# Four banks for the masked products of a recurrent chunk, its recurrence in one run, and the router within the output projection

## The reference

```python
def wkv7_scan(r, w, k, v, a, b):
    ...
        sa = jnp.einsum('bhij,bhj->bhi', state, a_t)
        state = (state * w_t[:, :, None, :] + sa[..., None] * b_t[:, :, None, :]
                 + v_t[..., None] * k_t[:, :, None, :])
        return state, jnp.einsum('bhij,bhj->bhi', state, r_t)
...
for i in range(DEPTH):
    ...
        mixed = jnp.concatenate([tok, mem_out.astype(tok.dtype)], axis=-1) @ w_out[i]
        x = layer_norm(DEEPNORM_ALPHA * x + mixed, ln1_g[i], ln1_b[i])
        ffn = moe_ffn(x.reshape(B_ * S_, D), w_router[i], router_bias[i], ...)
        x = layer_norm(DEEPNORM_ALPHA * x + ffn, ln2_g[i], ln2_b[i])
# in moe_ffn:
    scores = jax.nn.sigmoid((x2 @ w_router).astype(jnp.float32))
    _, idx = lax.top_k(scores + router_bias.astype(jnp.float32), TOP_K)
    ...
    shared = (jax.nn.silu(x2 @ w_sh_gate) * (x2 @ w_sh_up)) @ w_sh_down
```

## Time and profile before

| | us |
|---|---|
| median of 3 runs | 2351.93 (2348.82 to 2356.43) |
| the profiled execution | 2349.78 |
| its span | 2348.0 |
| PE busy | 2004.9 (85%) |
| DVE busy | 828.0 (35%) |
| DMA, mean rate | 230 GB/s |

### The profile page before, as it was taken

The page is one execution under the profiler, slowest core; times in us unless marked ns, Lnnn a source line. Parts: engine busy times, 40 slices in busy tenths (PEclk is TensorE's granted clock), DMA queues, the critical chain, the costliest instruction groups (busy, mean ns, idle before and its releaser), DMA issues. The chain is left out here.

```text
span 2348.0 us, 33222 instructions
## 1 busy us (share of the span) xinstructions
PE 2004.9 (85%) x11180; PEld 1226.0 (52%) x11181; DVE 828.0 (35%) x2198; ACT 361.7 (15%) x814; POOL 289.8 (12%) x375
## 2 busy tenths in 40 slices
PE   8999998798989887878897688988779897888885
PEld 5475545365655555533444377763446564554552
DVE  2001645422223222272545743313523232222236
ACT  1001631011101100012334211110101010100010
POOL 5000000011111111100134131000011111111110
PEclk9999999799989999998998599879889899998998
DMA  6211003699999999861222100002758999999966
GB/s 210 77 54 39 34 19 151 239 365 421 414 418 379 412 421 421 347 232 50 59 54 50 23 2 1 1 1 90 284 188 326 421 395 410 412 421 421 417 279 250
DMA packets 143456, 540.51 MB, mean 230 GB/s; under 512 B 30854, under 2 KB 68286, under 8 KB 93590
## 3 DMA queue, kind: packets, MB, share of 16 engines
q1 hardware_dynamic: 122070, 489.14, 52.0%
q0 software_dynamic: 21312, 50.37, 5.7%
HBM read 521.07 MB, written 45.61 MB: 241 GB/s over the span
## 5 line engine op out<-in xcount | busy, mean ns | idle before, releaser
L594 PE MATMUL bank<-W,XT 128*64 128x256 f32 x4608 | 569.1, 409 | 116.2 <-DMA W<-in_w_exp_up_dram 108.0
L594 PEld LDWEIGHTS bank<-W,XT 128*64 128x64 f32 x4608 | 413.2, 148 | 296.7 <-issue 197.9
L629 PE MATMUL bank<-W,ht 128*64 128x512 f32 x1152 | 263.1, 597 | 12.2 <-DVE ht L618 12.0
L647 POOL DMA_INDIRECT y_rows<-y,row x72 | 72.9, 1013 | 943.1 <-DVE y L640 943.1
L605 DVE TENSOR_TENSOR gu<-sig,bank 128x256 f32<-128x256 f32 x72 | 30.4, 422 | 409.5 <-ACT sig L601 409.5
L1733 PE MATMUL bank<-XT,rin_w 128*128 128x512 f32 x352 | 161.5, 615 | 0.0
L629 PEld LDWEIGHTS bank<-W,ht 128*64 128x64 f32 x1152 | 90.9, 136 | 127.0 <-issue 127.0
L1087 PE MATMUL bank<-XT,foxw 128*128 128x512 f32 x320 | 139.9, 599 | 0.0
L1733 PEld LDWEIGHTS bank<-XT,rin_w 128*128 128x128 f32 x352 | 68.6, 198 | 88.7 <-issue 88.4
L535 DVE TENSOR_TENSOR onehot<-rank,iota_s 128x128 bf16 x320 | 71.9, 287 | 97.9 <-issue 97.9
L601 ACT ACTIVATE sig<-bank 128x256 f32<-128x256 f32 x72 | 27.7, 384 | 508.5 <-PE bank L594 508.5
(11 more groups left out here) (390 smaller groups left out, 2395.9 us busy)
## 6 DMA issues: line engine op xcount, KB each, us to landing
W<-in_w_exp_gate_dram SPq DMA_DIRECT2D x128, 1024.0 KB, 14.6
W<-in_w_exp_up_dram SPq DMA_DIRECT2D x128, 1024.0 KB, 19.2
W<-in_w_exp_down_dram SPq DMA_DIRECT2D x128, 1024.0 KB, 17.9
W<-y_rows SPq DMA_DIRECT2D x16, 1536.0 KB, 17.6
foxw<-in_fox_w_in_dram SPq DMA_DIRECT2D x13, 1024.0 KB, 5.5
rin_w<-in_rwkv_w_in_dram SPq DMA_DIRECT2D x22, 512.0 KB, 4.0
w_out<-in_w_out_dram SPq DMA_DIRECT2D x1, 4096.0 KB, 13.2
x_rows<-X SPq DMA_DIRECT2D x2, 2048.0 KB, 16.4
```

The costliest lines, as they stand in the source:

```text
L594: last = pe.matmul((gate, up)[m][64 * a:64 * a + 64, :], xt[s][:, k, 64 * a:64 * a + 64], K.W[:, w, a, m, k * FE:(k + 1) * FE], start=(k = ...
L629: last = pe.matmul(B[5 + half][64 * a:64 * a + 64, :], ht[:, j, 64 * a:64 * a + 64], K.W[:, w, a, 2, at:at + 512], start=(j == 0), stop=(j ...
L647: pool.indirect_dma_start(out=K.y_rows, out_offset=bass.IndirectOffsetOnAxis(ap=row[s][:], axis=0), in_=y[s][:], in_offset=None, bounds_ch ...
```

## The change

Four things.

1. `a_products` puts pairs of heads in turn into banks 3 and 4 and banks 5 and 6 (`mask_bank`). A pair waits for the masks of the pair before the last.
2. In iteration c PE does z, the L products, deviations, u, variances, state and y, and then x5, spread, bonus, tw5, gate and x6. The lists of ACT and DVE are put in the same order.
3. Transposes and logits move from routing into the output projection, tile by tile, with `TileTurner` through banks 0 and 1 and logits in bank 2. Tile 0 is transposed before the products of tile 3; the others follow the products. The router's weights and the layer norm's vectors lie in the arena, and X is stored by tiles.
4. The shared expert's gate and down weights are loaded in the output projection (`SharedExpert`), so that routing loads only the router's bias and the up weights before the experts' weights.

```diff
@@ routed_experts_tables, sync
-                sp.dma_start(w_router[:], K.in_["w_router"][L].rearrange("(p k) e -> p k e", k=KD)).then_inc(loaded, 16)
                 sp.dma_start(bias[:, 0, :], K.in_["router_bias"][L:L + 1, :].broadcast_to([P, E])).then_inc(loaded, 16)
-                sp.dma_start(w_sh[:, 0, :], K.in_["w_sh_gate"][L].rearrange("(p k) f -> p (k f)", k=KD)).then_inc(loaded_sh, 16)
-                sp.dma_start(w_sh[:, 1, :], K.in_["w_sh_up"][L].rearrange("(p k) f -> p (k f)", k=KD)).then_inc(loaded_sh, 16)
-                shared.load(sp)
-                sp.dma_start(K.x_rows.rearrange("(t p) d -> p t d", p=P), X[:]).then_inc(stored, 16)
+                sp.dma_start(w_up[:], K.in_["w_sh_up"][L].rearrange("(p k) f -> p (k f)", k=KD)).then_inc(up_loaded, 16)
...
@@ routed_experts_tables, vector
-                dve.wait_ge(loaded, 32)
+                dve.wait_ge(loaded, 16)
                 dve.wait_ge(negexp_done, 1)
...
@@ TileTurner.turn
         pe.wait_ge(ln.done, 2 * t + 2)
+        if t:
+            pe.wait_ge(self.by_act, 2 * t)
...
@@ output_projection, sync
                 ln.load(sp)
+                sp.dma_start(router, K.in_["w_router"][L].rearrange("(p k) e -> p k e", k=KD)).then_inc(router_loaded, 16)
+                shared.load(sp)
+                for t in range(NT):
+                    sp.wait_ge(ln.done, 2 * t + 2)
+                    sp.dma_start(K.x_rows[t * P:(t + 1) * P, :], X[:, t, :]).then_inc(K.x_stored, 16)
@@ output_projection, tensor
+                def logits(t):
+                    tiles.await_tile(pe, t)
+                    if t == 0:
+                        pe.wait_ge(router_loaded, 16)
+                    for k in range(KD):
+                        pe.matmul(B[2][:, t * E:(t + 1) * E], K.XT[:, k, t * P:(t + 1) * P], router[:, k, :],
+                                  start=(k == 0), stop=(k == KD - 1))
...
+                    if t == 2:
+                        tiles.turn(pe, ln, 0)
+                logits(0)
+                for t in range(1, NT):
+                    tiles.turn(pe, ln, t)
+                    logits(t)
@@ output_projection, scalar
                 for t in range(NT):
                     ln.root(act, t)
+                    if t == NT - 2:
+                        tiles.copy(act, 0)
+                for t in range(1, NT):
+                    tiles.copy(act, t)
@@ rwkv_chunks
+        def mask_bank(h):
+            return B[3 + 2 * (h // 2 % 2) + h % 2]
...
         def a_products(pe, n, h0):
-            for h in (h0, h0 + 1):
-                if h >= 2:
-                    pe.wait_ge(a_kept, n * NH + h - 1)
-                elif n >= 2:
-                    pe.wait_ge(outs, n - 1)
-                elif n:
-                    pe.wait_ge(tok_k, 4 * n)
+            if h0 >= 4:
+                pe.wait_ge(a_kept, n * NH + h0 - 2)
+            elif n and h0 == 2:
+                pe.wait_ge(y_kept, 2 * n)
+            elif n >= 2:
+                pe.wait_ge(outs, n - 1)
+            elif n:
+                pe.wait_ge(tok_k, 4 * n)
@@ rwkv_chunks, tensor, iteration c
-                    if n < NT:
-                        x5(n)
                     u(c)
                     if c:
                         variances(c - 1)
                     if n < NT:
-                        tw5(n)
+                        state(c)
+                    y(c)
+                    if n < NT:
+                        x5(n)
                     if c:
                         spread_rstd(c - 1)
+                        bonus(c - 1)
                     if n < NT:
-                        state(c)
-                    if c:
-                        bonus(c - 1)
-                    y(c)
-                    if n < NT:
-                        x6(n)
+                        tw5(n)
                     if c:
                         gate(c - 1)
                     if n < NT:
+                        x6(n)
@@ rwkv_chunks, vector, iteration c
-                    for q in range(2 * GROUPS):
-                        if n < NT:
-                            add_tw5(n, q)
-                        if c and q == 1:
-                            invert_root(c - 1)
                     if c:
-                        scale_deviations(c - 1)
+                        invert_root(c - 1)
                     if n < NT:
                         update_state(c)
                     if c:
+                        scale_deviations(c - 1)
                         add_bonus(c - 1)
+                    if n < NT:
+                        for q in range(2 * GROUPS):
+                            add_tw5(n, q)
+                    if c:
                         gate_out(c - 1)
```

More of the change, by code:

```diff
@@ L283, in _, with shared_products @@
                             load_expert(K, sp, L, 2 * i + a, i, a, m)
-                sp.wait_ge(stored, 16)
+                sp.wait_ge(K.x_stored, 16 * NT * (L + 1))
             @block.tensor
             def _(pe):
-                for k in range(KD):
-                    if k >= 4:
-                        pe.wait_ge(xt_a if k % 2 == 0 else xt_d, (k - 4) // 2 + 1)
-                    for t in range(NT):
-                        last = pe.transpose(B[k % 4][:, t * P:(t + 1) * P], K.Xk[:, t, k, :], ident[:])
-                    last.then_inc(turned, 1)
-                pe.wait_ge(loaded, 32)
-                pe.wait_ge(xt_a, KD // 2)
-                pe.wait_ge(xt_d, KD // 2)
-                for t in range(NT):
-                    for k in range(KD):
-                        last = pe.matmul(B[4][:, t * E:(t + 1) * E], XT[:, k, t * P:(t + 1) * P], w_router[:, k, :],
-                                         start=(k == 0), stop=(k == KD - 1))
-                last.then_inc(logits, 1)
-                pe.wait_ge(loaded_sh, 32)
-                def shared_products(gu, j):
-                    for k in range(KD):
-                        last = pe.matmul(B[gu * 2 + j][:], w_sh[:, gu, k * FE + j * P:k * FE + (j + 1) * P],
+                def shared_products(gu, j):
+                    weights = w_up if gu else shared.gate
+                    if gu:
+                        pe.wait_ge(up_loaded, 16)
+                    else:
+                        pe.wait_ge(shared.gate_loaded, 16)
+                    for k in range(KD):
+                        last = pe.matmul(B[gu * 2 + j][:], weights[:, k * FE + j * P:k * FE + (j + 1) * P],
                                          XT[:, k, :], start=(k == 0), stop=(k == KD - 1))
@@ L346, in _ @@
             def _(act):
-                for k in range(0, KD, 2):
-                    act.wait_ge(turned, k + 1)
-                    act.activation(XT[:, k, :], B[k % 4][:], ACT.Copy).then_inc(xt_a, 1)
-                act.wait_ge(logits, 1)
-                act.activation(negexp[:], B[4][:, 0:NT * E].rearrange("p (t e) -> p t e", t=NT), ACT.Exp, scale=-1.0).then_inc(negexp_done, 1)
+                act.activation(negexp[:], B[2][:, 0:NT * E].rearrange("p (t e) -> p t e", t=NT), ACT.Exp, scale=-1.0).then_inc(negexp_done, 1)
                 for j in range(2):
@@ L1179, in fox_layer @@
         attention(K, L, pairs, dict(qT=qT, kT=kT, v=v, sgT=sgT, qmT=qmT, probT=probT), w_out)
-        output_projection(K, L, w_out)
+        shared = SharedExpert(K, L)
+        output_projection(K, L, w_out, shared)
+    return shared
 class BlockSolver:
@@ L1493, in _ @@
                     ln.normalize(dve, X[:, t, :], t)
+                tiles.copy_last(dve)
 C0 = float(np.exp(-0.5))
@@ L1568, in rwkv_layer @@
         w_out = OutWeights(K, scope, L)
-        output_projection(K, L, w_out, True)
+        shared = SharedExpert(K, L)
+        output_projection(K, L, w_out, shared, True)
+    return shared
 class RwkvWeights:
@@ L2342, in _ @@
                     keep_y(c)
+                    if n < NT:
+                        keep_x5(n)
                     if n < NT:
```

59 lines of the change are left out of this document (32 added, 27 removed).

## The result

The changed kernel takes 2318.38 us (median of 4 runs, 2313.81 to 2323.58) against 2351.19 us before (4 runs); the ratio of the two is 0.9858, 95% interval 0.9831 to 0.9885. The forecast was 2320. In a later series the same kernel took 2313.59 us (6 runs) against 2352.08 (22 runs), ratio 0.9836 (0.9812 to 0.9861). The profiled execution took 2313.81 us, the fastest of its four.

What follows compares the result with a forecast made beforehand. Ahead of the expert loops PE's waits were taken to count nearly in full. Terms 16.6 + 7.1 + 1.5 + 1.2 + 0.5 + 4 = 30.9 us from 2349.8 give 2318.9, said as 2320 for the median; range 2306 to 2338.

Steps and rivals of the forecast that it cites:

- The bound: Layer 1's expert loop starts at PE's pace; before the loops each wait on PE counts nearly in full.
- Masks, chunks 1 to 3: Masked products with four banks: PE's waits for the masks go, 8.0 us per chunk remain; 16.6 us saved.
- Chunk 0: Masked products at the end of the attention phase: transposes start and the phase ends 7.1 us earlier.
- The order: New order within a chunk: 1.5 us saved in iteration 0, 1.2 in 1 and 2 together, 0.5 in 3.
- the step of iteration 3: Y covers the 1.52 us wait for square root and reciprocal, gate waits about 1.1 us; 0.5 us saved.
- The 0.6 us of iteration 1: The 1.82 us wait for the gated output goes, a 1.20 us wait at the bonus comes; 0.6 us saved.
- Routing: Transposes and logits moved ahead of the barrier: 1.8 to 2.0 us saved a layer, 4 us for both.
- The load was the release: Sign: DVE's first addition in routing should be released by the bias load, not by the exponential.
- 2329 for a cold tail in one layer: Rival: routing gives nothing, 2324 us, or 2329 with one layer's tail cold; milder forms within the forecast's 0.55.
- The light stretches: Rival: U, variance, state, Y and the projection's tails run at a fallen clock; all cold, 2367 us, chance 0.04.
- The clock holds better: Rival: chunk 0's masks reach full clock, iteration 3 recovers early, bias lands at 2.4 us; 2308 us, chance 0.15.

Runs made afterwards that it cites:

- early bias: Changed kernel with the router bias loaded behind the shared weights in the output projection, plus one early exponential there; 2313.51 us, ratio 0.9838.
- Y behind the bonus: Changed kernel with Y of iteration 3 made after the spread and the bonus, as before the change; 2319.68 us, ratio 0.9860; traced again, 2319.07 us.
- dealt products: Early bias kernel with PE's four shared-expert products cut into pieces and placed in its waits during routing; 2301.52 us, ratio 0.9774.

## Why the prediction came out right

The mechanism was right for the masks and the routing. That the median, 2318.38, lies so near to 2320 is in part luck: the two traces differ by 35.9 us where the sum has 30.9, and the second series of the changed kernel is 38.5 us ahead of before. The terms that were too small are named below.

**The bound** was as read: each wait of PE ahead of the loops counts nearly in full. The three parts add up to the whole within their intervals, and of 36.9 us ahead of layer 1's loop 35.9 reach the end.

**Masks, chunks 1 to 3:** forecast 16.6, measured 17.6, and the banks alone give it. The stage is 7.7 us and not 8.0, since two pairs behind each other take 1.51 us where 1.70 was written (the solver products take 1.09 where 0.96 was). That chunk 3 would be back at full clock was right, but the reason given, that only the gaps distinguished it, fell: with the three gaps within it left and the new order it runs at full clock as well, and chunks 1 and 2 had the same gaps at full clock before. What set its clock stays open. **Chunk 0:** 7.1 and 7.1, though by two errors that cancel: the transposes start 8.5 us earlier at a higher clock, and POOL's expansion, which I let shift with the rest, now ends the phase.

**The order** was the mis-sized term: 1.5 + 1.2 + 0.5 = 3.2 us, measured 7.5 by the trace of before and after (10.7 by the second trace of the change) and 5 to 14 by the runs of the order alone. The waits came out as written: 1.52 gone, 1.20 and 1.11 come. What failed is the step of iteration 3, "0.5 saved": it counted waits and left the clock where it had been. Equal starts give 3.7 us for Y's place, 3.2 of them clock; the remaining 3.2 us of the 6.9 go with the clock coming back within U. Up to U eleven traces have the new order, and it came back there in six of them; with the old one it did in none of three. Since the same code up to there has it both ways, how much of this belongs to the order is not settled. The 0.6 us of iteration 1 did not come either: it lost 2.5, by half clock at the bonus and before.

**Routing:** forecast 2 a layer, measured 3.0 and 3.2. From the projection's start DVE's first addition comes 2.6 us sooner where 1.5 was written, though the bias took 4.0 to 4.4 us to land and not 3.5: the tail itself gained 6.3 us up to the shared products, not 4.3, since a tile's eight transposes took 1.10 us at full clock where 1.46 was written. The load was the release, as said. Among the rivals, 2329 for a cold tail in one layer does not follow from its own terms: 11 us on 2324 give 2335. **The last group norm** had no term, and lost 1.4 us to a gate at half clock and to the landing of w_out.

**The rivals.** The light stretches did not go cold as a whole; the bonus of iteration 1 did. The logits and transposes of the tail, 11.03 us of work in 14 with three waits of 0.73 to 1.07 us, ran at 1.00 throughout:

```profile
1619.00:1633.00 14.00, 11.03 (x90) 10.11 (x88) 6.45 (x10) 2.86 (x6) 0.00 (x0) 1.00 0.09 37
```

The Trainium skill's "TensorE: Matmul & The Clock Gate", "Part 4: PE-mode transpose", says that full clock does not engage for transposes. The earlier trace rows show it rise within them; the tail shows only that it holds over groups of eight (1.10 us each) with logit products between them, from a projection that ended at full clock. "The clock holds better" came true for iteration 3 and chunk 0, not for the bias; the second series of the changed kernel, 2313.6, lies between its 2308 and the forecast.

## What to carry to other kernels

Where two engines hand a buffer to and fro and neither is full, more buffers are worth the whole wait, here 3.7 us of idle time and 4.7 us of a stage's 12.4 each time; but find out which engine comes last once they stand free, for it was a third one (POOL) in chunk 0. Taking away the wait that ends last is worth only the distance to the next: the early bias gave 1 us in layer 1 where PE, just behind, needed 15.5 us for its shared products, and 2.8 where it needed 13.9. Independent matrix work is worth cutting into pieces, one behind every hand-over of the serial chain; this gave 12 us.

## What the runs showed of the hardware

The clock falls to half during the Z products of iteration 3 in all fourteen traces, whatever stands ahead, and stays there from 10 us (the changed kernel) to 27 us (the kernel before; Y behind the bonus with U at half). The same instructions then take 31.4 us (the changed kernel, early bias) or 38.7 (dealt products). The one kernel that was traced twice with the same starts to 0.1 us repeated all stages of the recurrence to 0.1 us; the changed kernel, traced twice with starts 1 to 2 us apart, took 47.4 and 44.1 us for iteration 1. So the start matters or goes with what matters; what decides is not shown. A difference under some 7 us between two single traces of this kernel is read stage by stage, and only stages whose clock agrees are compared.
